# Seven-product down chunks earlier in each feed-forward of a decoder trunk, and the memory's parts in an earlier turn

## What is computed

```python
D_MODEL = 1024; SEQ = 256; MEM_LEN = 256; D_FF = 2816; DEPTH = 2
def swiglu(h, w_gate, w_up, w_down):
    return (jax.nn.silu(h @ w_gate) * (h @ w_up)) @ w_down
# layer l:  x += 1/2 * swiglu(rms(x)); x += mixer(rms(x))
#           x += cross_attention(rms(x), rms(mem)); x += 1/2 * swiglu(rms(x))
```

## Time and profile before

| | |
|---|---|
| median of 3 runs | 1174.61 us (1174.28 to 1174.8) |
| the profiled execution | 1174.84 us, its span 1172.7 us |
| PE busy | 1165.1 us, 99% of the span, 6754 matmuls |
| DVE busy | 979.0 us, 83% |
| ACT busy | 747.1 us, 64% |
| POOL busy | 141.5 us, 12% |
| DMA | 202 GB/s in the mean |
| chain that ended last | PE 99% |

### The profile page before, as it was taken

How to read it: one execution, slowest core, us unless ns; L and a number is a source line. 1 busy time by engine, 2 the same in 40 slices (tenths; PEclk the granted TensorE clock), 3 DMA queues, 4 the chain that set the end, 5 groups by cost and what they waited for, 6 DMA issues and landing times.

```text
span 1172.7 us, 17754 instructions
## 1 busy us (share of the span) xinstructions
PE 1165.1 (99%) x6754; PEld 1019.4 (87%) x6754; DVE 979.0 (83%) x1134; ACT 747.1 (64%) x960; POOL 141.5 (12%) x139
## 2 busy tenths in 40 slices
PE   9999999999999999999999999999999999999998
PEld 8888889889989888888888888889887898888886
DVE  6689997875657589999988999997886676899997
ACT  7567766854457566777565777564576566677773
POOL 1000021520142010110010011010012121101000
PEclk9999999999999999999999999999999999999999
DMA  9957985454445455899755799846623334669991
GB/s 316 338 193 215 247 255 179 145 181 143 144 144 180 144 181 184 252 264 274 226 196 179 218 261 262 263 144 214 210 90 133 134 119 158 231 206 266 273 260 57
DMA packets 170056, 236.88 MB, mean 202 GB/s; under 512 B 15504, under 2 KB 139792, under 8 KB 169872
## 3 DMA queue, kind: packets, MB, share of 16 engines
q1 hardware_dynamic: 163664, 213.30, 55.5%
q0 software_dynamic: 6192, 22.55, 9.6%
q10 hardware_dynamic: 144, 0.26, 0.1%
HBM read 213.02 MB, written 1.05 MB: 183 GB/s over the span
## 4 chain that ended last, share of the span: by engine, by line
PE 99%; DMA 0%; DVE 0%; POOL 0%; issue 0%; POOLq 0%; ACT 0%; DVEq 0%; SPq 0%; ACTq 0%
PE ps L2302 30%; PE ps L2309 16%; PE ps L2281 15%; PE ps L2282 14%; PE ps L2283 14%; PE ps L2384 1%; PE ps L2569 1%; PE ps L3033 1%; PE ps L2889 1%; PE ps L3056 0%; PE ps L2577 0%; DMA arena<-in_first 0%; PE ps L2994 0%; PE ps L2991 0%; PE ps L2452 0%; PE ps L2641 0%
## 5 line engine op out<-in xcount | busy, mean ns | idle before, releaser
L2302 PE MATMUL ps<-hT,w_parts 128*128 128x512 f32 x1568 | 374.9, 391 | 0.9 <-DVE hT L1416 0.9
L2302 PEld LDWEIGHTS ps<-hT,w_parts 128*128 128x128 f32 x1568 | 290.1, 188 | 59.1 <-DVE w_parts L1443 0.7
L1374 DVE TENSOR_TENSOR w_parts<-raw,w_parts 128x2048 fp32r<-128x2048 f32 x85 | 195.9, 2314 | 57.9 <-ACT w_parts L758 57.8
L758 ACT ACTIVATE w_parts<-raw 128x2048 fp32r<-128x2048 f32 x85 | 162.3, 1920 | 73.5 <-PE ps L2283 71.0
L2309 PEld LDWEIGHTS ps<-hT,w_parts 128*128 128x128 f32 x1568 | 201.4, 191 | 8.0 <-DVE w_parts L1450 0.2
L2309 PE MATMUL ps<-hT,w_parts 128*128 128x256 f32 x1568 | 204.1, 283 | 0.0
L898 ACT ACTIVATE w_parts<-raw 128x2048 fp32r<-128x2048 f32 x79 | 150.9, 1910 | 1.0 <-DMA raw<-in_ffn_w_gate 1.0
L1592 DVE TENSOR_TENSOR w_parts<-raw,w_parts 128x2048 fp32r<-128x2048 f32 x58 | 132.5, 2284 | 0.4 <-ACT w_parts L898 0.4
L2236 POOL DMA_DIRECT2D xn<-arena x42 | 36.5, 868 | 503.7 <-ACT arena L909 503.7
L2281 PE MATMUL ps<-w_parts,hT 128*128 128x512 f32 (+1 forms) x240 | 91.0, 379 | 0.0
L2283 PE MATMUL ps<-w_parts,hT 128*128 128x512 f32 (+1 forms) x240 | 90.1, 375 | 0.0
(11 more groups left out here) (365 smaller groups left out, 2176.4 us busy)
## 6 DMA issues: line engine op xcount, KB each, us to landing
raw<-in_ffn_w_down SPq DMA_DIRECT2D x44, 1024.0 KB, 6.8
raw<-in_ffn_w_gate SPq DMA_DIRECT2D x43, 1024.0 KB, 5.2
raw<-in_ffn_w_up SPq DMA_DIRECT2D x43, 1024.0 KB, 6.4
xn<-arena POOLq DMA_DIRECT2D x42, 512.0 KB, 6.9
raw<-in_xattn_wkv SPq DMA_DIRECT2D x16, 1024.0 KB, 5.4
raw<-in_even_w_in SPq DMA_DIRECT2D x13, 1024.0 KB, 5.0
raw<-in_xattn_wq SPq DMA_DIRECT2D x8, 1024.0 KB, 5.1
raw<-in_xattn_wo SPq DMA_DIRECT2D x8, 1024.0 KB, 4.9
```

Of the source, the lines that this page charges most:

```text
L758: ins = nc.scalar.activation(hi, src, ACT.Copy)
L1374: ins = V.tensor_tensor(lo, src, hi.bitcast(F32), ALU.subtract)
L2302: mm(ps[:, bank0 + m, :], cols(w_hi, n, k, CW, m * P, (m + 1) * P), hT[:, k, :, :].rearrange("p a c -> p (a c)"), start=k == 0, stop=False)
```

## The change

Chunks 2 to 8 of f = 0 and 0 to 8 of the others are done in seven products: 34 in place of 29, two more in feed-forward 0 and one more, the first, in each of the three later ones. For chunk 0 of these the sums of the weight blocks and of the hidden blocks are written into the start of the feed-forward, ahead of the loop. In feed-forward 0 the memory's parts move to the turn of chunk 2, which is now a seven-product turn, and the squares to the turn of chunk 3; ACT waits for all of the memory's low parts (`turned_done`) before that turn, ahead of its gate copy, because that turn is the first to write kept copies into `xn`. PE's first product into a bank now overwrites it (`fresh`), and in the three later feed-forwards bank 6 is first written by the ordinary chunk 9. The number of POOL's adding DMAs is two per seven-product turn from the third on: 42 before, 52 after.

```diff
         class Mixed:
-            TURN, COUNT = (4, 1, 1, 1), (5, 8, 8, 8)
+            TURN, COUNT = (2, 0, 0, 0), (7, 9, 9, 9)
...
                     turn(0)
-                    turn(1)
+                    turn(1, True)
                     with sp.Fori(2, FJ - 1) as j:
                         turn(j, True)
...
                     silu(0)
+                    act.wait_ge(w_summed, w_sums_at(f, 0) + 2)
                     hi_upto(base + 5)
-                    hidden(f * FJ + 1, gu_hi)
+                    forms(0)
+                    act.wait_ge(w_summed, w_sums_at(f, 0) + 4)
+                    nc.scalar.activation(Mixed.w_hi, Mixed.w_sums, ACT.Copy).then_inc(w_sums_hi, 1)
...
                     turn(1)
-                    turn(2)
...
-                    turn(3, lambda c: mem_hi(range(3 * c, min(3 * c + 3, KT))))
-                    turn(4, lambda c: c and squares(1, mem_rows, lambda t, h: act.wait_ge(mem_in, 16), tiles=(c - 1,)),
-                         mixed=0)
-                else:
-                    turn(1, mixed=0)
+                    turn(2, lambda c: mem_hi(range(3 * c, min(3 * c + 3, KT))), mixed=0)
...
+                def memory_squares(c):
+                    if c:
+                        squares(1, mem_rows, lambda t, h: act.wait_ge(mem_in, 16), tiles=(c - 1,))
+
                 first = Mixed.TURN[f]
-                turn(first + 1, mixed=1, out=0)
+                if f == 0:
+                    act.wait_ge(turned_done, 2 * KT)
+                turn(first + 1, memory_squares if f == 0 else lambda c: None, mixed=1, out=0)
                 turn(first + 2, mixed=2, out=1, added=True)
...
                     gate_sum(j)
                     gate_scale(j)
                     split(base + 2 + RING)
+                    between(0)
                     up_sum(j)
                     product(j)
                     dve.wait_ge(mult_done, j + (f * FJ + 1))
...
+                    gu_sums(i)
                     n, m = base + 4 + RING, (base + 4) % RING
                     dve.wait_ge(raw_in[m], (j - 1) * 16 + landed(n))
...
                     split(base + 3 + RING)
+                    between(1)
                     w_sum(i, 2, Mixed.w_sums[:, 1, :], slot[:, 2, :], slot[:, 0, :], ALU.subtract)
                     forms_low(j)
                     w_sum(i, 3, Mixed.w_sums[:, 2, :], slot[:, 3, :], Mixed.w_sums[:, 1, :], ALU.subtract)
...
                     V.tensor_tensor(Mixed.w_lo, Mixed.w_sums, Mixed.w_hi.bitcast(F32), ALU.subtract).then_inc(lo_done, 1)
+                    between(2)
...
                 else:
+                    n, m = base + 4, (base + 4) % RING
                     lo_upto(base + 3)
                     gate_sum(0)
+                    dve.wait_ge(raw_in[m], landed(n))
+                    w_sum(0, 0, Mixed.w_sums[:, 0, :], slot[:, 2, :], slot[:, 0, :], ALU.add)
+                    dve.wait_ge(w_summed, w_sums_at(f, 0) + 1)
+                    w_sum(0, 1, slot[:, 0, :], slot[:, 1, :], slot[:, 0, :], ALU.subtract)
                     lo_upto(base + 4)
                     up_sum(0)
+                    w_sum(0, 2, Mixed.w_sums[:, 1, :], slot[:, 2, :], slot[:, 0, :], ALU.subtract)
+                    w_sum(0, 3, Mixed.w_sums[:, 2, :], slot[:, 3, :], Mixed.w_sums[:, 1, :], ALU.subtract)
...
                     product(0)
-                    lo_upto(base + 5)
-                    hidden_lo(0, gu_hi, gu_lo)
+                    dve.wait_ge(mult_done, f * FJ + 1)
+                    gu_sums(0)
+                    dve.wait_ge(hi_done, n + 1)
+                    V.tensor_tensor(w_lo[:, m, :], raw[:, m, :], w_hi[:, m, :].bitcast(F32),
+                                    ALU.subtract).then_inc(down_split, 1)
+                    forms_low(0)
+                    dve.wait_ge(w_sums_hi, w_sums_hi_at(f, 0) + 1)
+                    V.tensor_tensor(Mixed.w_lo, Mixed.w_sums, Mixed.w_hi.bitcast(F32), ALU.subtract).then_inc(lo_done, 1)
+                first = Mixed.TURN[f]
                 if f == 0:
                     turn(1)
-                    turn(2)
-                    turn(3, lambda c: mem_lo(range(3 * c, min(3 * c + 3, KT))))
-                first = Mixed.TURN[f]
-                turn_mixed(first, 0)
+                    turn_mixed(first, 0, lambda c: mem_lo(range(3 * c, min(3 * c + 3, KT))))
                 with dve.Fori(1, Mixed.COUNT[f]) as i:
...
                                         cols(w_lo, n, k, D, h * 512, (h + 1) * 512),
-                                        first and k == 0, final and k == 1)
+                                        (first or (t, h) in fresh) and k == 0, final and k == 1)
...
                         pe.wait_ge(up_read, j + (f * FJ + 1))
                     last = product3(ps[:, bank, :], a[0][:, ai, :], a[1][:, ai, :], b[0][:, bi, :], b[1][:, bi, :],
-                                    alone, alone)
+                                    alone or fresh, alone)
...
                         pe.wait_ge(gu_done, j + f * FJ)
-                        used(mixed_down(n + 2, f, j, mixed))
+                        used(mixed_down(n + 2, f, j, first))
                         pe.wait_ge(mixed_read, mixed * 2 + (mixed_read_at(f, 0) + 1))
                         return
...
-                    hidden_down(j + f * FJ, n + 2, first, False)
-
-                turn(1, True)
+                    hidden_down(j + f * FJ, n + 2, first, False, fresh=fresh)
...
                 first = Mixed.TURN[f] + 1
                 if f == 0:
+                    turn(1, True)
                     with pe.Fori(2, first) as j:
                         turn(j, False)
-                turn(first, False, mixed=0)
+                    turn(first, False, mixed=0)
+                else:
+                    turn(1, True, mixed=0)
                 with pe.Fori(1, Mixed.COUNT[f]) as i:
                     turn(i + first, False, kept=i, mixed=i)
-                turn(FJ - 1, False, held=f == 3, kept=Mixed.COUNT[f])
+                turn(FJ - 1, False, held=f == 3, kept=Mixed.COUNT[f], fresh=((1, 0),) if f else ())
                 n = base + FFN_CHUNKS - 1
```

21 lines of the change are left out of this document (11 added, 10 removed).

## The result

The changed kernel takes 1178.13 us in the median of 12 runs (1174.94 to 1179.75), the kernel before 1174.63 (1174.28 to 1174.93): ratio 1.0026, 95% interval 1.0018 to 1.0034. It is slower by 3.5 us, where no change to speak of was forecast (1174.9, range 1171.1 to 1177.2). The runs of before lie within 0.65 us of each other, those of the changed kernel within 4.8. That is a result too, and the experiments come back to it.

The account below looks back on a forecast made before the run. PE was taken to bound the kernel, busy 1165.1 of 1172.7 us. Its saving of 3.43 against stalls of 2.17, 0.61, 0.2, 0.49 and 0.14 gave +0.2 on 1174.61, hence 1174.9 us, range 1171.1 to 1177.2.

Parts of the forecast that it names:

- the model of the turn: Seven-product turns: PE takes 15.90 us, DVE 15.73 without a gap, so DVE wins back only 0.17 a turn.
- the three starts: First turns of the three later feed-forwards: PE stalls 0.64, 0.32 and 1.21 us for DVE, +2.17 in all.
- Landing + 14.40 − start of the down chunk: Stall rule at the later starts: DVE's chain of 17.83 us from down 0's landing, less PE's 3.43 to its need.
- The term of 0.32: Start of f = 2: stall of 0.32 us, from down 0's load taking 5.5 us.
- rival B: Loop turns: late down loads cost PE 0.27 us a turn over some 22 turns, +6, 1180.8; chance 0.08.
- the tails: Last hidden part of the first and last feed-forward: DVE late beyond its slack, stalls of +0.49 and +0.14 us.
- the squares: Feed-forward 0, turn after the first converted one: ACT squares the memory's rows between its copies, +0.2 us.
- the first turn: Feed-forward 0, chunk 2 with the memory's parts: `up_sum` ready at 67.16, needed at 66.55, stall +0.61 us.
- A: Whole kernel: DVE's order has an unseen gap, so all 3.43 us stay saved, 1171.2; chance 0.12.
- A′: First turns: DVE's steps come out 0.1 shorter, half the saving stays, 1172.7 to 1173.7; chance 0.20.
- C: First turns: DVE waits for ACT's longer order, 1 us lost in each start, 1177.9; chance 0.08.
- E: Four first turns: short waits drop PE's clock from 2.4 to 1.2 GHz, +19 us, 1194; chance 0.02.

Follow-up runs that it names:

- e1: The changed kernel with feed-forward 0 put back as before, so only the three later feed-forwards converted; 1176.52 us, ratio 1.0016 to the kernel before.
- e4: Feed-forward 0 as before, the three later ones changed, with the low part of up 1 ahead of the wait for down 0; 1173.39 us, ratio 0.9989.
- e9: The kernel before with the two small strided loads (`pe_pairs`) issued twice in the same place; 1177.35 us, ratio 1.0023.
- e8: The changed kernel with the later feed-forwards as before and the two strided loads issued in the mixer; 1174.33 us, ratio 0.9998 to the kernel before.
- e12: The kernel with only the later feed-forwards changed, plus a redundant low part of up 1 in each of their starts; 1190.05 us, ratio 1.0132.

## Why the prediction was wrong

**Right: the model of the turn.** DVE's seven-product turn is as long as PE's less 0.17, and the table of leads shows it: from 0.39 to 1.57 in seven turns, 0.17 each. "The change pays PE's saving back as waits for DVE at exactly the turns that it converts" held in part. Four of the five converted turns pay it back, two of them more than twice; the turn of chunk 3 keeps all of its 0.69; and 2.55 of the 7.27 us of stalls stand in turns that the change does not convert.

**Right, sized within 0.25: the three starts.** Landing + 14.40 − start of the down chunk, with this execution's own landings (426.04, 611.88, 1001.45) and starts without a stall (439.99, 624.70, 1014.55), gives 0.45, 1.58 and 1.30; measured 0.70, 1.82 and 1.50. (A landing is the start of the first weight sum less 0.05.) This is the rule worked out anew with what the result showed, not the forecast. Some 0.2 to 0.25 each were missing: PE was 0.57 us late at the first down chunk of f = 1, ahead of bank 0, and 0.13 more behind it, where I had counted one wait, at bank 2.

**Wrong: "The three loads ... take 5.8, 5.5 and 4.7 us".** The earlier trace rows I took the durations of one execution for the load's own. That of f = 2 took 5.5 in the profile of before, 6.8 in that of after, 7.2 in e1 and 6.7 in e4, and each tenth goes straight to PE. The term of 0.32 measured 1.82. That is 1.5 of the 3.6 us between the sum's +0.2 and the +3.84, 1.3 of it by the landing alone. In the kernel before, where DVE did not wait for this load ahead of the low part of up 1, the same kind of scatter cost nothing: its 33 runs beside e1 to e4 lie within 0.64 us.

**Missing: a term for what SP's queue does to the gate load of f = 0.** I weighed late *down* loads as rival B, at 0.44 a turn, and asked only for the mean. What came was one gate load, issued 1.9 us and landed 3.0 us later than before, behind two small strided loads, once in the kernel: 1.90 + 0.65 = 2.55, and the sum had nothing for it. My sum had the lateness ("about 1.86 − 4 × 0.17 = 1.18 later at its end") and used it for the tail alone, without asking how near each *load* already was to being waited for; ACT's 0.63 for gate 9's stood in the trace of before and would have told. B's pair of conditions was right (no lead, and a late landing), the load was another one: within the seven-product loops DVE waited for a down load once, 0.81 us at 132.18, and PE did not feel it. e9 shows that a late gate load is enough, without any edit of the change. This term and that of f = 2 are 4.05 us, more than the 3.6 that were missing; the three other stalls are 0.4 larger than forecast, and the terms of the next paragraph, 0.8, did not come. Neither large term is the turn's own cost: both are loads that a chain without its lead has to wait for.

**Too much: the tails and the squares.** The forecast +0.49 and +0.14 for the last hidden part and +0.2 for the squares are not there: chunk 3 to 4 has its whole 0.69, e8's chunk 9 follows without a stall, and f = 3 loses nothing in the changed kernel. The lateness in the sum was too large: in e8 the lead at chunk 8 is 0.98 and was 1.49, so that DVE is 0.51 later there and not 1.18, within the slack of 0.69; and in f = 3 the ordinary turn of chunk 9 brings the lead back to 1.86, as before. For f = 0 the first turn was 0.70, forecast 0.61.

So by place: forecast 0.61 + 0.2 + 0 + 0.49 in f = 0, measured 0.70 + 0 + 2.55 + 0; forecast 0.64, 0.32, 1.21 and 0.14 later, measured 0.70, 1.82, 1.50 and 0.

**Rivals.** A (all cover holds) and A′ fell. C (ACT's order) fell: from the landing of down 0 to PE's wait no low part waited for ACT, and `product` waited 0.70 for `silu`, as counted. E (the clock) was not in the changed kernel's profile, where the clock was 1.00, but its mechanism is real: e1 and e12 show it, at 1.6 to 2.7 us a time and not 19 in all: it came with some of the long waits only, and lasted 3 to 7 us. (The prediction took the span's 1.00 for a sign that no stretch was lower. The same row of e1 has 1.00 too.) The changed kernel's slowest run, 1179.75, has the lowest mean clock of the twelve, 0.997 against 0.998 and 0.999; that it had such a fall is likely, not shown.

**The range** had the wrong thing in it: ends for the steps of DVE, none for the landings. Had each of the three landings and the gate load been given a microsecond, its upper end would have been some 4 us higher, 1181, and held the result.

## What to carry to other kernels

An engine at 83% of the span looks as if it had room. What it really has is its lead where the bounding engine waits for it, 1.86 us here, and this lead is also the buffer that keeps the scatter of DMA out of the time. Before spending it on extra work, list every load that the engine's chain meets and how near each is to being waited for, and take the spread of its durations over several places or executions, not one row. Where a wait for a load must be in an in-order queue, put everything that doesn't need the load ahead of it (here 2.2 us of work, worth 3.1 us of the median and 2.8 of 3.4 us of scatter, e1 to e4). The version with three converted chunks and that order (1173.39) beats the one with five (1178.13).
